# A gated linear recurrence with its decay taken as an exponential, and its gates kept as tanh, in a two-block transformer kernel

## The chip, the core and the metric

The kernel runs on one core of one Trainium2 chip. The metric is the device time of one execution in microseconds (us). TensorE (PE) does the matrix products, ScalarE (ACT) the activation functions and copies, VectorE (DVE) the elementwise work and scans, GpSimd (POOL) one kind of subtraction, SyncE (SP) starts the loads. Every engine works through its own queue in order, and the engines meet only at semaphores.

## What is computed

The program is a chain of blocks over 256 tokens of width 1024: a hybrid mixer with a gated FFN, a recurrent mixer, two expert layers, an attention mixer. The change lies in the recurrent mixer alone:

```python
xb, gb = jnp.split(h @ in_w, 2, axis=-1)
xb = causal_depthwise_conv(xb, conv_w, conv_b)
r = sigmoid(einsum('bsnc,ncd->bsnd', xblk, ra_w) + ra_b)
i = sigmoid(einsum('bsnc,ncd->bsnd', xblk, ri_w) + ri_b)
log_a = -8.0 * softplus(-lam) * r
a = jnp.exp(log_a)
u = jnp.sqrt(-jnp.expm1(2.0 * log_a)) * (i * xb)
hs = scan(h_t = a_t * h_{t-1} + u_t)
y = hs * gelu(gb);  return y @ out_w
```

The width of the recurrence is 1408 channels, so 11 tiles of 128 channels by 256 tokens (`RT` is 11).

## The kernel before

Weights are float32 and every product is made in three passes: a weight tile is split into a `high` part (rounded to float32r) and a `low` part (the rest). SP loads a tile of 128x1024 into one of four slots of `ring`. ACT copies it to `high` (line 1439, called through `ahead`), POOL subtracts to get `low` (line 1767), and PE multiplies (line 787): 16 matmuls with `high`, 8 with `low`. There are three buffers for split tiles, so the splitting runs at most three tiles ahead of PE.

In the recurrent stage PE goes, for each tile j from 0 to 10, through the product x_j, the two gate products of tile j - 2 (`lru_gates`, line 794, into the PSUM tensor `ms`, four banks in turn), and the product g_j. After the loop come the gates of tiles 9 and 10, then 48 matmuls of one column for a later stage (`sum_mods`), and then the output product `lru_out`, whose first two half tiles wait until 8 tiles of y are done, the third until all 11 are.

DVE does the causal convolution of x_j (`lru_conv`, four operations, ended by a memset that signals), then `lru_low(j - 6)`, `lru_coefficients(j - 2)` and `lru_scan(j - 5)`. After the loop it does the coefficients of tile 9, scans and lows of tiles 6 to 8, the coefficients of tile 10, and the rest. PE's gate products of tile j wait for the convolution of tile j + 1 and for the coefficients of tile j - 2 (semaphore `lru_gates_used`).

ACT does for each j the splits, `lru_high(j - 6)` (the rounded copy of a finished y), `lru_act(j - 2)` (the gate functions), the evacuation of g_j (line 1448), and after tiles 2, 5, 8 and 10 `lru_roots`, a square root and a gelu over the tiles finished so far. At the end it does the gate functions of tiles 9 and 10, two splits for `lru_out`, `lru_high` of 5 to 8, the last roots, and `lru_high` of 9 and 10.

The decay is written without an exponential: with t = tanh(4 * softplus(-lam) * r), the kernel uses a = 2 / (1 + t) - 1 and sqrt(1 - a*a) = 2 * sqrt(t) / (1 + t). The factor `c5` comes from `lru_rate`, a chain of small operations on DVE over 128x11, which stands in front of the third tile of the FFN's first product, long before the recurrent stage. `c3` in it is softplus(-lam). `S.settle()` waits for the engine's own last result; `S.did` signals it. `ts`, `tt` and `stt` are DVE's tensor_scalar, tensor_tensor and scalar_tensor_tensor, recorded under lines 1803, 1800 and 1806.

## Time and profile before

| | |
|---|---|
| median of 3 runs | 2595.98 us |
| lowest, highest | 2595.3, 2599.94 us |
| the profiled execution | 2597.65 us |
| its span | 2595.9 us |
| PE busy | 2484.1 us, 96% |
| DVE busy | 1758.1 us, 68% |
| ACT busy | 1225.7 us, 47% |
| POOL busy | 1227.1 us, 47% |
| recurrent stage, with its output product | about 570 to 717 us of the span |

All times of the trace are microseconds from the start of the span. A row of the timeline shows the start, the length, the engine, the line, the operation, and in brackets how long the engine sat idle in front of it and what ended that. Matmul ends are modelled, so the busy share of PE is no measure of its peak.

### The profile page before, as it was taken

Reading aid. Unit: us, or ns where it says so; the run is one execution under the profiler, and the core shown is the slowest. Engines: PE = TensorE matmul, PEld = TensorE weight load, DVE = VectorE, ACT = ScalarE, POOL = GpSimd, SP = SyncE. Lnnn points to the kernel's source line nnn. Section 1 sums busy time; section 2 is a strip of 40 time slices with the busy share of each in tenths; the row PEclk is TensorE's granted clock in tenths of the full one; section 3 lists DMA queues with packets and bytes.
Section 4 is the critical chain, followed back from the end, with each engine's and each line's share of the span. In section 5 each row is a group of like instructions: output and inputs, shape, how many; then the busy total and the mean of one; then the engine's idle time right before and its main releaser. Section 6 shows DMA issues by size and latency. Waiting matters only on the chain.

```text
span 2595.9 us, 46935 instructions
## 1 busy us (share of the span) xinstructions
PE 2484.1 (96%) x18074; PEld 2295.9 (88%) x18074; DVE 1758.1 (68%) x3289; ACT 1225.7 (47%) x2091; POOL 1227.1 (47%) x506
## 2 busy tenths in 40 slices
PE   7899899989799999999999999999999999999999
PEld 7899899979789999998888888888999999888887
DVE  4558553467619969996767765651996899655555
ACT  5325433446445544444444444544545444454544
POOL 4437577745459987771000004446898777200000
PEclk8899899989899999999999997999999999999999
DMA  4325576743245565556777763334556555566664
GB/s 159 98 72 171 205 261 238 293 180 121 89 144 179 181 185 155 155 155 222 257 253 258 259 227 98 106 99 154 171 171 187 155 155 156 176 191 193 190 192 146
DMA packets 125918, 457.93 MB, mean 176 GB/s; under 512 B 13968, under 2 KB 15376, under 8 KB 125584
## 3 DMA queue, kind: packets, MB, share of 16 engines
q1 hardware_dynamic: 125424, 450.73, 54.1%
q10 hardware_dynamic: 288, 4.33, 0.4%
q8 instruction: 145, 2.38, 0.4%
q14 instruction: 61, 0.50, 0.1%
HBM read 453.95 MB, written 1.05 MB: 175 GB/s over the span
## 4 chain that ended last, share of the span: by engine, by line
PE 78%; DVE 7%; POOL 6%; issue 6%; ACT 3%; DMA 1%; SPq 0%; POOLq 0%; DVEq 0%; ACTq 0%
PE ms L1257 27%; PE mm L787 21%; PE mm L1217 19%; POOL low L1767 6%; PE ms L1238 3%; PE ms L794 1%; DMA ring<-w_ple_gate 1%; PE mm L794 1%; DVE hs L1806 1%; PE mm L802 1%; PE mm L900 1%; DVE scratch L1806 1%; DVE work L1800 0%; PE ms L999 0%; DVE work L1806 0%
## 5 line engine op out<-in xcount | busy, mean ns | idle before, releaser
L1767 POOL TENSOR_TENSOR low<-ring,high 128x1024 fp32r<-128x1024 f32 (+2 forms) x502 | 1226.9, 2456 | 1002.7 <-ACT high L1439 844.6
L1646 ACT ACTIVATE high<-ring 128x1024 fp32r<-128x1024 f32 x506 | 535.9, 1059 | 357.0 <-PE ms L1257 325.9
L1217 PE MATMUL mm<-hs,high 128*128 128x256 f32 x4096 | 521.8, 280 | 3.4 <-ACT high L1439 3.4
L1257 PE MATMUL ms<-high,wts 128*128 128x512 f32 x2048 | 511.1, 392 | 0.0
L1217 PEld LDWEIGHTS mm<-hs,high 128*128 128x128 f32 x4096 | 488.2, 188 | 3.8 <-issue 3.8
L2313 DVE TENSOR_TENSOR low<-ring,high 128x1024 fp32r<-128x1024 f32 x256 | 313.3, 1225 | 248.2 <-ACT high L1646 248.2
L1257 PEld LDWEIGHTS ms<-high,wts 128*128 128x128 f32 x2048 | 384.2, 188 | 83.3
L787 PE MATMUL mm<-hs,high 128*128 128x256 f32 x2608 | 346.9, 288 | 4.6 <-DVE parts L1800 4.4
L1439 ACT ACTIVATE high<-ring 128x1024 fp32r<-128x1024 f32 (+2 forms) x252 | 258.0, 1030 | 184.1 <-PE mm L787 111.1
L787 PEld LDWEIGHTS mm<-hs,high 128*128 128x128 f32 x2608 | 326.4, 196 | 9.1 <-issue 7.5
L1217 PE MATMUL mm<-hs,low 128*128 128x256 f32 x2048 | 276.1, 277 | 11.9 <-POOL low L1767 11.8
L1257 PE MATMUL ms<-low,wts 128*128 128x512 f32 x1024 | 275.7, 391 | 3.0 <-DVE low L2313 3.0
L1217 PEld LDWEIGHTS mm<-hs,low 128*128 128x128 f32 x2048 | 251.9, 188 | 14.6 <-POOL low L1767 14.5
L1257 PEld LDWEIGHTS ms<-low,wts 128*128 128x128 f32 x1024 | 192.1, 188 | 46.2 <-DVE low L2313 3.8
L787 PE MATMUL mm<-hs,low 128*128 128x256 f32 x1304 | 179.0, 280 | 0.4 <-POOL low L1767 0.4
L1654 ACT ACTIVATE mm<-mm 128x256 f32<-128x256 f32 (+47 forms) x148 | 39.6, 267 | 269.5 <-PE mm L1217 269.5
L787 PEld LDWEIGHTS mm<-hs,low 128*128 128x128 f32 x1304 | 164.6, 191 | 0.7 <-POOL low L1767 0.7
L2278 DVE TENSOR_TENSOR onehots<-onehots,ms 128x512 bf16<-128x512 bf16 x256 | 162.8, 676 | 0.0
L1448 ACT ACTIVATE work<-mm 128x256 f32<-128x256 f32 (+2 forms) x145 | 60.3, 417 | 204.9 <-PE mm L787 167.9
L1656 ACT ACTIVATE work<-mm 128x256 f32<-128x256 f32 (+17 forms) x248 | 79.7, 321 | 152.6 <-PE mm L1217 152.5
L787 PE MATMUL mm<-parts,high 128*128 128x256 f32 x896 | 126.8, 294 | 15.9 <-DVE parts L1800 10.3
L787 PEld LDWEIGHTS mm<-parts,high 128*128 128x128 f32 x896 | 117.0, 198 | 18.6 <-DVE parts L1800 10.8
(316 smaller groups left out, 2796.1 us busy)
## 6 DMA issues: line engine op xcount, KB each, us to landing
ring<-w_peer_experts SPq DMA_DIRECT2D x512, 512.0 KB, 3.6
work<-w_mod SPq DMA_DIRECT2D x48, 512.0 KB, 4.6
ring<-w_late_mods SPq DMA_DIRECT2D x48, 512.0 KB, 4.6
ring<-w_ffn_up SPq DMA_DIRECT2D x44, 512.0 KB, 3.8
ring<-w_peer_q SPq DMA_DIRECT2D x32, 512.0 KB, 3.6
ring<-w_fox_in SPq DMA_DIRECT2D x32, 512.0 KB, 3.6
ring<-w_lru_in SPq DMA_DIRECT2D x22, 512.0 KB, 3.6
ring<-w_gates SPq DMA_DIRECT2D x16, 512.0 KB, 3.6
```

Source lines behind the costliest of these rows:

```text
L787: ins = pe.matmul(dst, l, r_, start=first and s_ == 0 and k == 0, stop=last and s_ == 2 and k == rows - 1, skip_group_check=True)
L794: ins = pe.matmul(dst, a, b, start=first and i == 0, stop=i == len(pairs) - 1, skip_group_check=True)
L1217: ins_ = pe.matmul(mm[:, s_ % BANKS, 0:T], w_[:, k * P:(k + 1) * P], hs[:, b_, k, :], start=pass_ == 0 and k == 0, stop=pass_ == 2 and k = ...
L1238: ins_ = pe.matmul(ms[:, 2 + i % 2, t * P:(t + 1) * P], onehot[:, i % 2, 3, t, :], onehot[:, i % 2, third, t, :], start=third == 0, stop=t ...
L1257: ins_ = pe.matmul(ms[:, 2 * c + half, :], wts[:, s_ % 3, b_, c * P:(c + 1) * P], v_[:, half * 512:(half + 1) * 512], start=s_ == 0 and pa ...
L1439: act.activation(high[0:rows, q % CUT, 0:width], ring[0:rows, n_ % RAW, 0:width], ACT.Copy) \
L1448: S.did(act.activation(dst, src, func), taken(n))
L1646: act.activation(high[:, (q0 + i) % CUT, :], ring[:, n_ % RAW, :], ACT.Copy) \
L1656: ins = act.activation(placed[:, s_, at:T], src[:, at:T], ACT.Gelu)
L1767: pool.tensor_tensor(low[0:rows, cut_slot, 0:width], ring[0:rows, raw_slot, 0:width], high[0:rows, cut_slot, 0:width].bitcast(F32), ALU.su ...
L2278: dve.tensor_tensor(onehot[:, k % 2, s], onehot[:, k % 2, 2], third(s), ALU.mult)
L2313: dve.tensor_tensor(low[:, q % CUT, :], ring[:, n % RAW, :], high[:, q % CUT, :].bitcast(F32), ALU.subtract).then_inc(sem("low_done"), 1)
```

## The change

The gates stay as tanh. With tr = tanh(z/2), the sigmoid is (1 + tr)/2, so the decay is a = exp(-4c - 4c*tr) with c = softplus(-lam): one ACT Exp with the same column as scale and bias (`lruc` column block 5, now times -4). It is made on ACT beside the tanh of the root, t = tanh(2c + 2c*tr), and goes straight into `la`. Since 1 + a = 2 / (1 + t), the factor in front of the input is sqrt(t/4) * (1 + a) * (1 + ti) * x, with ti the tanh of the input gate. DVE makes (1 + ti) * x in place in PSUM and multiplies by (1 + a). Three small operations in `lru_rate` make the new columns.

```diff
@@ lru_act
-                S.did(act.activation(lr[:, j, :], lru_gate(0, j), ACT.Sigmoid, bias=v("ra_b", j, j + 1)))
+                S.did(act.activation(lr[:, j, :], lru_gate(0, j), ACT.Tanh, bias=lruc[:, 6, j:j + 1], scale=0.5))
                 act.wait_ge(sem("lru_gated"), 2 * j + 2)
-                S.did(act.activation(lru_gate(1, j), lru_gate(1, j), ACT.Sigmoid, bias=v("ri_b", j, j + 1)))
-                S.settle()
-                S.did(act.activation(lt[:, j, :], lr[:, j, :], ACT.Tanh, scale=lruc[:, 5, j:j + 1]), "lru_tanh")
+                S.did(act.activation(lru_gate(1, j), lru_gate(1, j), ACT.Tanh, bias=lruc[:, 7, j:j + 1], scale=0.5))
+                S.settle()
+                S.did(act.activation(lt[:, j, :], lr[:, j, :], ACT.Tanh, bias=lruc[:, 8, j:j + 1],
+                                     scale=lruc[:, 8, j:j + 1]))
+                S.did(act.activation(la[:, j, :], lr[:, j, :], ACT.Exp, bias=lruc[:, 5, j:j + 1],
+                                     scale=lruc[:, 5, j:j + 1]), "lru_decay")
@@ lru_roots
-                act.wait_ge(sem("lru_t_read"), e + 1)
-                S.did(act.activation(lt[:, first:e + 1, :], lt[:, first:e + 1, :], ACT.Sqrt), "lru_root")
+                S.settle()
+                S.did(act.activation(lt[:, first:e + 1, :], lt[:, first:e + 1, :], ACT.Sqrt, scale=0.25), "lru_root")
@@ lru_rate
-                ts(c5, c3, 4.0, None, ALU.mult, None, "lru_rate")
+                ts(lruc[:, 6, :], v("ra_b"), 0.5, None, ALU.mult)
+                ts(lruc[:, 7, :], v("ri_b"), 0.5, None, ALU.mult)
+                ts(lruc[:, 8, :], c3, 2.0, None, ALU.mult)
+                ts(c5, c3, -4.0, None, ALU.mult, None, "lru_rate")
@@ lru_coefficients
-                dve.wait_ge(sem("lru_tanh"), j + 1)
-                r_, i_ = lru_gate(0, j), li[:, j, :]
-                ts(lr[:, j, :], lt[:, j, :], 1.0, None, ALU.add, None, "lru_t_read")
-                S.settle()
-                S.did(dve.reciprocal(r_, lr[:, j, :]))
-                tt(i_, lru_gate(1, j), lc[:, j, :], ALU.mult)
-                S.settle()
-                stt(i_, r_, 2.0, i_, ALU.mult, ALU.mult)
-                ts(la[:, j, :], r_, 2.0, -1.0, ALU.mult, ALU.add, "lru_gates_used")
+                dve.wait_ge(sem("lru_decay"), j + 1)
+                gate = lru_gate(1, j)
+                stt(gate, gate, 1.0, lc[:, j, :], ALU.add, ALU.mult)
+                S.settle()
+                stt(li[:, j, :], la[:, j, :], 1.0, gate, ALU.add, ALU.mult, "lru_gates_used")
```

ACT's queue at the end of the loop, from the evacuation of g_10 to the gate functions of tile 10. Lines 1598 and 1599 are the root and the gelu (1601 and 1602 after the change); 1583, 1585 and 1587 are the gate functions and the tanh of the root, 1589 after the change is the Exp. Before:

```order
L1448 ACTIVATE work<-mm 128x256
L1598 ACT_TABLE_LOAD
L1598 ACTIVATE work<-work 128x768
L1599 ACT_TABLE_LOAD
L1599 ACTIVATE work<-work 128x768
L1583 ACT_TABLE_LOAD
L1583 ACTIVATE work<-ms,vec 128x256
L1585 ACTIVATE ms<-ms,vec 128x256
L1587 ACTIVATE work<-work,lruc 128x256
L1583 ACTIVATE work<-ms,vec 128x256
L1585 ACTIVATE ms<-ms,vec 128x256
L1587 ACTIVATE work<-work,lruc 128x256
```

After:

```order
L1602 ACT_TABLE_LOAD
L1602 ACTIVATE work<-work 128x768
L1583 ACTIVATE work<-ms,lruc 128x256
L1585 ACTIVATE ms<-ms,lruc 128x256
L1587 ACTIVATE work<-work,lruc 128x256
L1589 ACT_TABLE_LOAD
L1589 ACTIVATE work<-work,lruc 128x256
L1583 ACTIVATE work<-ms,lruc 128x256
L1585 ACTIVATE ms<-ms,lruc 128x256
L1587 ACTIVATE work<-work,lruc 128x256
L1589 ACTIVATE work<-work,lruc 128x256
```

One activation is added for each tile, and the table load behind the gelu has moved from the first gate function to the Exp. In the whole stage there are 12 table loads in both programs.

DVE's queue from the coefficients of tile 9 through the scan of tile 6 (lines 2196 and 2198 are the scan itself). Before:

```order
L1803 TENSOR_SCALAR work<-work 128x256
L2183 RECIPROCAL ms<-work 128x256
L1800 TENSOR_TENSOR work<-ms,work 128x256
L1806 SCALAR_TENSOR_TENSOR work<-ms,work 128x256
L1803 TENSOR_SCALAR work<-ms 128x256
L1800 TENSOR_TENSOR work<-work 128x256
L2196 SCALAR_TENSOR_TENSOR work<-work 128x256
```

After, from the scan of tile 8 and the low of tile 7 through the coefficients of tile 10:

```order
L1803 TENSOR_TENSOR work<-work 128x256
L2198 SCALAR_TENSOR_TENSOR work<-work 128x256
L1803 TENSOR_TENSOR work<-work 128x256
L1803 TENSOR_TENSOR parts<-work,parts 128x256
L1809 SCALAR_TENSOR_TENSOR ms<-ms,work 128x256
L1809 SCALAR_TENSOR_TENSOR work<-work,ms 128x256
```

Five operations of a coefficient step have become two; scans and lows stand as they stood. The queues of PE and SP are the same in both programs, and POOL's in its operations.

## Rows read from the trace of the kernel before

**Rows 1.** Windows: length, busy of PE, PEld, DVE, ACT, POOL, PEclk, DMA share, GB/s
```profile
660.00:680.00 20.00, 11.39 (x75) 11.13 (x76) 16.83 (x27) 11.71 (x18) 4.83 (x2) 0.68 0.12 37
```

**Rows 2.** Timeline of PE in the recurrent stage; L794 are gate products
```profile
615.12 2.75 PE L794 MATMUL ms<-work 128*128 128x256 f32 x12
...
631.41 2.75 PE L794 MATMUL ms<-work 128*128 128x256 f32 x12
...
639.37 1.21 PE L787 MATMUL mm<-hs,low 128*128 128x256 f32 x8 [0.36 <-POOL low L1767]
...
649.22 2.86 PE L794 MATMUL ms<-work 128*128 128x256 f32 x12 [0.59 <-DVE tiny L2174]
...
656.53 2.86 PE L794 MATMUL ms<-work 128*128 128x256 f32 x12 [1.71 <-DVE tiny L2174]
660.07 1.97 PE L794 MATMUL ms<-work 128*128 128x256 f32 x8 [0.67 <-DVE work L1803]
...
675.94 3.79 PE L787 MATMUL mm<-parts,high 128*128 128x256 f32 x16 [8.55 <-DVE parts L1800]
```

**Rows 3.** Timeline of DVE: first operation of a coefficient step, first of the next scan
```profile
649.42 0.29 DVE L1803 TENSOR_SCALAR work<-work 128x256 f32<-128x256 f32 x1
...
652.74 0.43 DVE L1800 TENSOR_TENSOR work<-work 128x256 f32<-128x256 f32 x1
```

**Rows 4.** Groups by form, DVE, 580 to 684: busy, mean ns, idle before
```profile
L2183 DVE RECIPROCAL ms<-work 128x256 f32<-128x256 f32 x11 | 19.4, 1761 | 0.4
...
L1806 DVE SCALAR_TENSOR_TENSOR work<-ms,work 128x256 f32<-128x256 f32 x11 | 4.7, 424 | 0.4
```

**Rows 5.** Groups of ACT: busy, mean ns, idle before
```profile
L1587 ACT ACTIVATE work<-work,lruc 128x256 f32<-128x256 f32 x11 | 5.6, 509 | 0.4
...
L1592 ACT ACTIVATE parts<-work 128x256 fp32r<-128x256 f32 x11 | 4.6, 415 | 30.6 <-DVE work L1800 30.6
```

**Rows 6.** Timeline of ACT from the evacuation of g_10 to the high of tile 5
```profile
655.95 0.36 ACT L1448 ACTIVATE work<-mm 128x256 f32<-128x256 f32 x1
656.33 1.28 ACT L1598 ACT_TABLE_LOAD   x1
...
663.19 0.46 ACT L1583 ACTIVATE work<-ms,vec 128x256 f32<-128x256 f32 x1
...
664.44 1.99 ACT L1439 ACTIVATE high<-ring 128x1024 fp32r<-128x1024 f32 x2
666.33 0.40 ACT L1592 ACTIVATE parts<-work 128x256 fp32r<-128x256 f32 x1
```

**Rows 7.** Timeline of DVE: scan of tile 6, lows of tiles 5 and 7
```profile
666.65 1.54 DVE L1800 TENSOR_TENSOR work<-work 128x256 f32<-128x256 f32 x1
668.22 2.71 DVE L2196 TENSOR_TENSOR_SCAN work<-work 128x256 f32<-128x256 f32 x1
...
671.31 0.42 DVE L1800 TENSOR_TENSOR parts<-work,parts 128x256 fp32r<-128x256 f32 x1
...
675.47 0.42 DVE L1800 TENSOR_TENSOR parts<-work,parts 128x256 fp32r<-128x256 f32 x1
```

**Rows 8.** Timeline of POOL beside it
```profile
665.55 4.83 POOL L1767 TENSOR_TENSOR low<-ring,high 128x1024 fp32r<-128x1024 f32 x2 [13.46 <-ACT high L1439]
```

**Rows 9.** Timelines of ACT and DVE: the last roots, and the scan behind them
```profile
676.01 1.28 ACT L1598 ACT_TABLE_LOAD   x1
...
679.97 0.43 DVE L1800 TENSOR_TENSOR work<-work 128x256 f32<-128x256 f32 x1 [0.65 <-ACT work L1599]
```

**Rows 10.** Timelines of DVE, PE and POOL at the end of lru_rate
```profile
334.97 0.17 DVE L1803 TENSOR_SCALAR lruc<-lruc 128x11 f32<-128x11 f32 x1
335.05 0.43 DVE L1800 TENSOR_TENSOR mm<-mm,work 128x256 f32<-128x256 f32 x1
...
336.54 3.39 PE L787 MATMUL mm<-hs,high 128*128 128x256 f32 x16 [4.41 <-DVE parts L1800]
...
337.84 2.38 POOL L1767 TENSOR_TENSOR low<-ring,high 128x1024 fp32r<-128x1024 f32 x1 [4.77 <-ACT high L1439]
```

More of the change, by code:

```diff
@@ L454, in build @@
         csilu = sb("csilu", [P, KD])
-        lruc = sb("lruc", [P, 6, RT])
+        lruc = sb("lruc", [P, 10, RT])
         tiny = sb("tiny", [P, 512])
```

## The prediction, made before the changed kernel ran

> **What bounds the kernel now.** I began with the page: PE is busy for 96% of the span, so only those stretches can give anything in which PE waits. The windows showed one around the recurrent stage: from 660 to 680 PE is busy 11.39 us of 20 and DVE 16.83 [rows 1]. I then read PE's own timeline there, and the reader is to look at the brackets [rows 2]. Until 637 PE never waits: two rounds of x, gates and g take 16.29 us (615.12 to 631.41). After that DVE is late: 0.59 and 1.71 us of waiting for convolutions, 0.67 for a coefficient step, and 8.55 us until the lows of tiles 0 to 7 are done. There is also one wait of 0.36 us for a split tile. Nothing else in the stage can be won, and of these waits the last is much the longest. So the question is not how much DVE saves but when the low of tile 7 comes, which lets PE go at 675.94.
>
> **Part 1, the coefficient step on DVE.** Before it takes 3.32 us (649.42 to 652.74) [rows 3], of which the reciprocal is 1.76 [rows 4]. After it is two operations of 0.42 us [rows 4] with some 0.03 between, 0.9 us. That frees 2.4 us a tile, 27 us over 11 tiles. Most of it falls where DVE is not waited for. What it surely does is end the backlog from 637 on: a round of DVE (convolution 2.2, low 0.4, coefficients 0.9, scan 1.7, with up to 2.7 of stalls) fits into 8.15.
>
> The new operations read one operand from PSUM and one from SBUF. I have no row of one that writes PSUM in place; the bounds are 0.42 (this row) and the 0.54 of a convolution's first operation, so 1.3 us more in all at worst, off the path but for 0.1 of tile 9. I take 0.42.
>
> **Part 2, ACT.** The Exp has two column operands, scale and bias. The tanh with one takes 0.509, a copy with none 0.415 [rows 5]; so I estimate 0.60 with two. The root's tanh goes from 0.51 to 0.60 too. Since neighbours overlap by some 0.1, a tile costs ACT 0.6 us more, 6.6 over the stage. Table loads stay 12. In most rounds ACT waits for PE or for DVE, which hides this; on the way to the low of tile 7 nothing hides it for tiles 9 and 10.
>
> The Trainium skill (ScalarE: Activation LUTs, What ACT_TABLE_LOAD costs) says that each such column operand adds some 93 ns; the rows show 94, so the price of the new form would be the same by either.
>
> **Part 3, the way to the low of tile 7.** Step by step:
> - PE. Without the waits the gates of tile 8 begin 16.29 after 631.41, at 647.70, instead of 649.22: 1.52 earlier. The gates of tile 9 began at 656.53 behind a wait of 1.71; without it they begin at 656.53 - 1.71 - 1.52 = 653.30 [rows 2]. The product g_10 stands just in front of them.
> - ACT. Its evacuation of g_10 came at 655.95, late because ACT had been waiting for a product of DVE. It now comes at about 653.3, 2.65 earlier. From there ACT's queue is solid: roots and gelu of tiles 6 to 8 with the gate functions of tile 9 (656.33 to 663.19), gate functions of tile 10 (to 664.44), two splits (to 666.33), then the high of tile 5 [rows 6]. That is 10.38 us, and two tiles at 0.6 make it 11.6. So the high of tile 5 begins at 664.9 and ends at 665.3.
> - DVE. The Exp of tile 9 is done at about 661.3 (663.3 - 2.65 + 0.7), its coefficients at 662.2, the scan of tile 6 at 663.9. Then DVE waits for that high until 665.3. Before, DVE came to this point at 671.31, behind everything else [rows 7].
> - The stalls. Operations of DVE that read two SBUF operands stand still while POOL works: the multiply at 666.65 took 1.54 instead of 0.43, and the scan at 668.22 took 2.71 instead of 0.69 [rows 7], under a pair of POOL operations from 665.55 to 670.38 [rows 8]. The pair begins when the first split of `lru_out` is done, so it moves by 2.65 - 1.2 to 664.1, its first half ends at 666.5, and the second at 668.9. The low of tile 5, ready at 665.3, is held to 666.7. The multiply of tile 7 then meets the second half and ends at 669.1. From there no POOL work is left. Unhindered, low 5 to low 7 is 4.16 us (671.31 to 675.47) and the first 0.97 of it are the low and the multiply, so 3.19 remain: low 7 begins at 672.3 against 675.47, **3.2 us earlier**.
>
> The Trainium skill (SBUF — State Buffer, Terms) says that DVE and GpSimd share one pair of SBUF ports under a lock held for the whole instruction, and that the loser is blocked. The rows agree. By that rule the sum is -3.2; were the stalls chance, it would be the -6.0 of the second rival.
>
> **Part 4, the tail.** The last roots begin behind the high of tile 8 at 676.01, and the scan of tile 9 waits for them to 679.97 [rows 9]. The high of tile 8 hangs on the scan of tile 8, so this moves by the same 3.2. The shorter coefficient step of tile 10 lies in this wait and gives nothing. After it the work is unchanged. PE has its wait in front of `lru_out` longer, not shorter: gates and column sums end at about 662.3 and it starts at 672.4. The 16 matmuls at 675.94 took 3.79 us for the usual 1.98, as the granted clock was at half there [rows 1, 2]; that cost remains.
>
> **Part 5, lru_rate.** Here DVE is waited for: PE stood 4.41 us until 336.54 for the operation behind this chain [rows 10]. The three added operations are of 0.17 us, but follow without a settle, like 334.97 and 335.05, so 0.08 each: **+0.25 us** straight on PE's path. A POOL operation beside them could hold each for up to its own 2.4 us, 7 in all, but POOL is idle there until 337.84, since its split comes from ACT, which waits for the same DVE work [rows 10]. I take 0.25.
>
> **Sum.** -3.2 + 0.25 = -2.95. The profiled execution took 2597.65 with a span of 2595.9, so its like would be 2594.7. It lies 1.7 above the median; taken from the median of 2595.98 the forecast is **2593.0 us**.
>
> **Rivals.**
> - *No stalls (17%).* POOL's pair and DVE's operations miss each other. Then low 5 goes at 665.3, low 7 4.16 later at 669.4: -6.0 + 0.25, **2590.2**. Against it: the two are both set off by ACT within 1.2 us of each other, and the pair lasts 4.83.
> - *One more stall (12%).* A third operation meets POOL, as where the scan lost 2.0 [rows 7]: -1.0 in all, **2595.0**.
> - *It does not do what it says (6%).* PE's last wait is set by ACT's queue in a way that I took too short: the load between tanh and Exp, or a dearer Exp, eats the 2.65. Then the low of tile 7 comes as before, **2596.2**.
> - *ACT becomes the bound, slower (5%).* A round without roots costs ACT some 4.8 us, one with roots and a reload 10.4, against PE's 8.15. If the three split buffers do not absorb these 2.2 us, PE waits in three rounds, and each wait can bring the half clock, as at 336.54 (3.39 for 1.98 us) [rows 10]: 3 x 3.6 - 2.95 = +7.9, **2603.9**. For it: the one wait of 0.36 for POOL [rows 2] came behind such a round. Against it: in that round ACT was late because it waited for DVE, which is now gone, and with three buffers it can run about a tile (24 matmuls, a third of a round) ahead. It decides from where ACT's lag passes that lead.
>
> **How the numbers follow.** The forecast has 60%. What a measurement of this kernel can tell from no change is about 0.2%, 5.2 us; so under 2590.8 counts as faster and over 2601.2 as slower. Faster is most of the first rival and the lower edge of the forecast's own spread (the runs before differ by 4.6, and the half clock costs some 2 us that may fall otherwise): 20%. Slower is the last rival and a little of disturbance: 6%. The rest is 74%. The range goes from 2589.0, under the case without stalls, to 2597.0, above the case in which nothing is won; the last rival and an odd run are left out.
>
> **What the trace would show.** Right: PE's waits of 0.59, 1.71 and 0.67 are gone; coefficient steps take 0.9 us; Exp takes 0.60; the first `lru_out` matmuls begin near 673.0 (675.94 - 3.2 + 0.25), behind an idle of PE of some 10 us instead of 8.55; DVE waits for an ACT high in front of a low, and one or two of its operations there last near 2 us. Wrong: PE's brackets name POOL `low` or ACT in the middle of the stage; the wait at 336.54 grows by over 1 us; or low 7 begins under 670, which would say that the stalls were misjudged.

## The result, and the profile after

The changed kernel takes 2660.86 us (median of 4 runs, 2658.92 to 2661.25) against 2597.96 for the kernel before in the same comparison: 1.0242 times as long, with an interval of 1.0226 to 1.0258. That is 63 us slower, where 3 us faster was forecast with a range up to 2597.0. The sign was wrong and the size was off by a factor of twenty, so the first question is where in the program the time went.

It did not go into the recurrent stage. Here is PE's timeline of that stage after the change, to be read against [rows 2]. The first row is the first gate product of the stage, which I take as the stage's zero from here on, since the stage begins at other times in other executions:

```profile
592.61 1.89 PE L794 MATMUL ms<-work 128*128 128x256 f32 x8
...
647.92 2.18 PE L787 MATMUL mm<-hs,high 128*128 128x256 f32 x16 [0.54 <-ACT high L1439]
...
660.55 2.86 PE L794 MATMUL ms<-work 128*128 128x256 f32 x12 [0.61 <-DVE tiny L2180]
...
667.67 4.58 PE L794 MATMUL ms<-work 128*128 128x256 f32 x20 [1.39 <-DVE tiny L2180]
...
687.20 3.78 PE L787 MATMUL mm<-parts,high 128*128 128x256 f32 x16 [8.16 <-DVE parts L1803]
```

From the first gate product to the first product of `lru_out` it is 94.59 us. Before it was 675.94 - 583.39 = 92.55, with the row of its first gate product:

```profile
583.39 1.89 PE L794 MATMUL ms<-work 128*128 128x256 f32 x8
```

So the stage is 2 us longer, of 63. The rest is everywhere. The page's groups of PE show it, first the kernel before, then the one after (busy us in all, mean ns of one, idle time before):

```profile
PE 2484.1 (96%) x18074; PEld 2295.9 (88%) x18074; DVE 1758.1 (68%) x3289; ACT 1225.7 (47%) x2091; POOL 1227.1 (47%) x506
...
L1217 PE MATMUL mm<-hs,high 128*128 128x256 f32 x4096 | 521.8, 280 | 3.4 <-ACT high L1439 3.4
L1257 PE MATMUL ms<-high,wts 128*128 128x512 f32 x2048 | 511.1, 392 | 0.0
```

```profile
PE 2555.8 (96%) x18074; PEld 2352.3 (88%) x18074; DVE 1744.2 (66%) x3259; ACT 1231.6 (46%) x2102; POOL 1226.6 (46%) x506
...
L1217 PE MATMUL mm<-hs,high 128*128 128x256 f32 x4096 | 543.8, 284 | 3.4 <-ACT high L1439 3.4
L1257 PE MATMUL ms<-high,wts 128*128 128x512 f32 x2048 | 521.7, 397 | 1.0 <-DVE wts L2306 1.0
```

The same 18074 matmuls take 71.7 us more; PE's idle time (span less busy) falls from 111.8 to 103.1, and 71.7 - 8.7 = 63.0 is the whole difference of the spans. Lines 1217 and 1257 are the expert layers; line 1217 runs from 782.6 us of the span to 2233.2, where the change does nothing. The two timelines there, at the full granted clock, show each matmul a little slower. Before, then after:

```profile
1003.76 2.09 PE L1217 MATMUL mm<-hs,high 128*128 128x256 f32 x16
1005.68 1.07 PE L1217 MATMUL mm<-hs,low 128*128 128x256 f32 x8
1006.60 0.84 PE L1238 MATMUL ms<-onehots 128*128 128x128 bf16 x12
```

```profile
1003.10 2.16 PE L1217 MATMUL mm<-hs,high 128*128 128x256 f32 x16
1005.10 1.12 PE L1217 MATMUL mm<-hs,low 128*128 128x256 f32 x8
1006.06 0.84 PE L1238 MATMUL ms<-onehots 128*128 128x128 bf16 x12
```

The 24 matmuls on `hs` go from 2.84 us (1003.76 to 1006.60) to 2.96 (1003.10 to 1006.06), while the 12 on `onehots` take 0.84 in both. A clock would have slowed both kinds. The measure that I use from here on is the **pitch**: the mean distance between the starts of neighbouring matmuls of one group in the trace, those at half clock left out. It went from 114.5 to 119.9 ns for line 1217 on `hs` and `high`, and from 229.1 to 234.3 for line 1257. Over all groups on `hs`, `parts` and `wts` the pitches make 77 us (4096 x 5.4 ns is 22 of them); the 71.7 measured are a little less. At half clock the matmuls did not get slower: the pitch of line 787 on `hs` is 213 ns there in both traces, and the 16 at 687.20 above took 3.78 us, those in [rows 2] 3.79. These matmuls are counted in the 77.

What the change does to the whole program is a line that the diff ahead of the prediction left out, since it seemed to be room for columns and nothing more:

```diff
-        lruc = sb("lruc", [P, 6, RT])
+        lruc = sb("lruc", [P, 10, RT])
```

`lruc` grows from 264 to 440 bytes a partition, and every tensor allocated behind it (`tiny`, `work` with `parts` in it, `hs`, `wts`) moves by 160 bytes in SBUF. `ring`, `high` and `low` stand ahead of it and stay. In bytes from the partition's start, as the two programs lay them out, `high` is at 17536 in both, and `hs` at 199488 before and 199648 after.

### The profile page after: what moved, and what is told of

It reads as the page before. It is cut to its first block, busy times and chain, and to the rows that moved or that the text cites. A ratio compares the mean times of both kernels' runs of the same rounds, so it can differ in the third digit from the quotient of the medians.

```text
span 2658.9 us, 46916 instructions
## 1 busy us (share of the span) xinstructions
PE 2555.8 (96%) x18074; PEld 2352.3 (88%) x18074; DVE 1744.2 (66%) x3259; ACT 1231.6 (46%) x2102; POOL 1226.6 (46%) x506
## 4 chain that ended last, share of the span: by engine, by line
PE 76%; DVE 7%; POOL 6%; issue 5%; ACT 3%; DMA 1%; SPq 0%; POOLq 0%; DVEq 0%; ACTq 0%
PE ms L1257 27%; PE mm L787 20%; PE mm L1217 19%; POOL low L1770 6%; PE ms L1238 3%; DMA ring<-w_ple_gate 1%; DVE work L1809 1%; DVE hs L1809 1%; DVE work L1803 1%; PE mm L802 1%; PE mm L794 1%; PE mm L900 1%; PE ms L794 1%; DVE scratch L1809 1%; ACT high L1439 1%
## 5 line engine op out<-in xcount | busy, mean ns | idle before, releaser
L1217 PE MATMUL mm<-hs,high 128*128 128x256 f32 x4096 | 543.8, 284 | 3.4 <-ACT high L1439 3.4
L1257 PE MATMUL ms<-high,wts 128*128 128x512 f32 x2048 | 521.7, 397 | 1.0 <-DVE wts L2306 1.0
L1217 PEld LDWEIGHTS mm<-hs,high 128*128 128x128 f32 x4096 | 507.4, 188 | 3.8 <-issue 3.8
L787 PE MATMUL mm<-hs,high 128*128 128x256 f32 x2608 | 359.3, 291 | 4.4 <-DVE parts L1803 3.8
L787 PEld LDWEIGHTS mm<-hs,high 128*128 128x128 f32 x2608 | 337.7, 196 | 8.8 <-issue 6.4
L1217 PE MATMUL mm<-hs,low 128*128 128x256 f32 x2048 | 287.6, 282 | 7.4 <-POOL low L1770 7.4
L1257 PE MATMUL ms<-low,wts 128*128 128x512 f32 x1024 | 281.6, 397 | 2.9 <-DVE low L2315 2.9
L1217 PEld LDWEIGHTS mm<-hs,low 128*128 128x128 f32 x2048 | 263.5, 188 | 9.5 <-POOL low L1770 9.5
L787 PE MATMUL mm<-hs,low 128*128 128x256 f32 x1304 | 185.9, 285 | 0.3 <-POOL low L1770 0.3
L787 PEld LDWEIGHTS mm<-hs,low 128*128 128x128 f32 x1304 | 170.8, 192 | 0.8 <-POOL low L1770 0.7
L787 PEld LDWEIGHTS mm<-parts,high 128*128 128x128 f32 x896 | 118.2, 196 | 16.4 <-DVE parts L1803 9.8
```

What stands on the lines that cost most here:

```text
L787: ins = pe.matmul(dst, l, r_, start=first and s_ == 0 and k == 0, stop=last and s_ == 2 and k == rows - 1, skip_group_check=True)
L1217: ins_ = pe.matmul(mm[:, s_ % BANKS, 0:T], w_[:, k * P:(k + 1) * P], hs[:, b_, k, :], start=pass_ == 0 and k == 0, stop=pass_ == 2 and k = ...
L1257: ins_ = pe.matmul(ms[:, 2 * c + half, :], wts[:, s_ % 3, b_, c * P:(c + 1) * P], v_[:, half * 512:(half + 1) * 512], start=s_ == 0 and pa ...
```

## The experiments

The two theories of the first round were **placement** (the 63 us come from where `hs`, `parts` and `wts` lie, whatever the arithmetic is) and **work** (the new instructions on ACT and DVE hold PE up). Within placement it was then **absolute** (a tensor's own address decides) against **distance** (the address of one operand of a matmul relative to that of the other). A matmul has two operands: the weights, which are loaded ahead of it, and the moving operand, of which the count of columns is told here (256 or 512).

### e1_room_only: the room without the change

```diff
 (the kernel before)
-        lruc = sb("lruc", [P, 6, RT])
+        lruc = sb("lruc", [P, 10, RT])
```

> The kernel before, with nothing changed but the size of lruc: 10 blocks of columns instead of 6, four of them unused. In the trace of the changed kernel the matmuls that read hs follow each other at some 120 ns instead of 113.4, from the first microseconds on, long before any changed operation runs. Theory P (placement): the larger lruc moves tiny, work, parts, hs and wts by 160 bytes in SBUF, from a multiple of 64 bytes to 32 bytes past one, and TensorE streams its moving operand slower from there. Then this kernel takes 2658 to 2664 us, like the changed one. Rival W (work): the new operations or the new order on ScalarE and VectorE slow TensorE; then it takes 2595 to 2600 us.

Measured: 2660.33 us (2657.02 to 2661.54), 1.0249 times the kernel before (1.0234 to 1.0264). The group in its page is that of the changed kernel to 0.1 us:

```profile
L1217 PE MATMUL mm<-hs,high 128*128 128x256 f32 x4096 | 543.7, 284 | 3.4 <-ACT high L1439 3.4
```

No instruction differs from the kernel before, so the whole loss is placement.

### e2_same_place: the change without the room

The new columns go into blocks 0, 1 and 2 of `lruc`, which nobody reads any more by then (the softplus is in block 3):

```diff
 (the changed kernel)
-        lruc = sb("lruc", [P, 10, RT])
+        lruc = sb("lruc", [P, 6, RT])
...
-                ts(lruc[:, 6, :], v("ra_b"), 0.5, None, ALU.mult)
-                ts(lruc[:, 7, :], v("ri_b"), 0.5, None, ALU.mult)
-                ts(lruc[:, 8, :], c3, 2.0, None, ALU.mult)
+                ts(lruc[:, 0, :], v("ra_b"), 0.5, None, ALU.mult)
+                ts(lruc[:, 1, :], v("ri_b"), 0.5, None, ALU.mult)
+                ts(lruc[:, 2, :], c3, 2.0, None, ALU.mult)
```

> The changed kernel whole, but its three new columns lie in blocks 0, 1 and 2 of lruc, whose old contents are used up by then; lruc keeps its 6 blocks and every tensor its place. Theory P: matmuls on hs go back to 113.4 ns, and only the forecast effects of the arithmetic remain: 2593 to 2596 us, 3 under the kernel before (low of tile 7 some 3.2 us earlier, lru_rate 0.25 longer); 2590 if the stalls of VectorE under GpSimd miss. Rival W: 2655 to 2662 us.

Measured: 2598.11 us (2591.42 to 2601.82, 12 runs), 1.0006 times before (0.9996 to 1.0016), which is 2 us above the 2593 to 2596 that I expected. Placement holds from this side too, and the theory of work falls. It is also the run that puts the prediction's own question, what the arithmetic is worth in the old order, and its answer is nothing that the runs can tell from zero: -1.0 to +4.2 us, where -2.95 was forecast. What became of them is taken up under e9.

### e3_room_pad32: 32 bytes more behind the larger lruc

```diff
 (the changed kernel)
         lruc = sb("lruc", [P, 10, RT])
+        gap = sb("gap", [P, 8])
```

> The changed kernel with lruc of 10 blocks, followed by an unused tensor of 32 bytes a partition. hs then starts at a multiple of 128 bytes (before: 64 past one). Theory P in the form 'multiple of 64 bytes': the time of e2, 2590 to 2597 us. If instead the exact old place matters, or the distance to other tensors, it stays at 2620 to 2662 us. If 128 bytes is the finer rule, it is below e2.

Measured: 2643.24 us (2640.74 to 2648.93), 1.0186 (1.0173 to 1.0199). The loss depends on the bytes themselves: 32 bytes more gave back 17 to 18 of 63 us. It is not a matter of being moved or not.

### e4_hs_moved and e5_all_moved: absolute or distance

```diff
 (e4: the kernel before)
+        gap = sb("gap", [P, 8])
         hs = sb("hs", [P, 2, KD, T], F32R)
```

> The kernel before, with an unused tensor of 32 bytes in front of hs: hs and wts lie 32 bytes past a multiple of 64, while tiny, work and parts stay. Theory P with the moving operand as its carrier: 6144 matmuls of line 1217 and 3912 of line 787 read hs and lose 6 ns each, 3072 of line 1257 read wts and lose some 4: 60 + 12 = 70 less what waits absorb, so 2650 to 2662 us. If it is work or parts that matter (the other engines' traffic), 2595 to 2605 us.

```diff
 (e5: the kernel before)
+        gap = sb("gap", [P, 8])
         ring = sb("ring", [P, RAW, SLOT])
```

> The kernel before with an unused tensor of 32 bytes a partition in front of everything: ring, high, low and all others lie 32 bytes further, and all distances between them stay. So hs lies 352 bytes past a multiple of 512 (before: 320), and high 160 (before: 128). Theory A (absolute place of the moving operand): matmuls on hs follow each other at 118 ns and more as when hs alone moved by 32, 2640 to 2665 us. Theory D (distance between the moving operand and the weights that are loaded beside it): pitch and time stay as before, 114.6 ns, 2594 to 2600 us.

e4 moves `hs` and `wts` (with `slots`, which shares the place of `wts`) by 32 bytes and nothing else: 2643.62 us, 1.0183 (1.0168 to 1.0198). e5 moves `hs` and `wts` by the same 32 bytes, and `high` and all others with them: 2594.28 (8 runs), 1.0002 (0.9991 to 1.0014). In both, `hs` lies at the same address, no multiple of 64. Their pages, e4 first (with the added line of code 1217 has become 1218, and 1257 is 1258):

```profile
L1218 PE MATMUL mm<-hs,high 128*128 128x256 f32 x4096 | 537.2, 284 | 3.4 <-ACT high L1440 3.4
L1258 PE MATMUL ms<-high,wts 128*128 128x512 f32 x2048 | 519.7, 395 | 0.0
```

```profile
L1218 PE MATMUL mm<-hs,high 128*128 128x256 f32 x4096 | 523.1, 280 | 3.4 <-ACT high L1440 3.4
L1258 PE MATMUL ms<-high,wts 128*128 128x512 f32 x2048 | 510.5, 391 | 0.0
```

So the distance between the two operands decides, and the absolute address does not. In e4 `parts` stayed where it was, and so did the pitch of its products (116.2 ns against 116.3): each pair of operands counts by its own distance. (Strictly, these two runs show that the distance to something among `ring`, `high` and `low` counts, as no run moved these against each other. That it is the other operand of the same matmul follows from the products with changed roles below.) The time of e4 is below the 2650 that I expected at least, so I had the size of one step wrong, not its sign.

### e6 to e8, e13 and e14: which distances

All five are e2_same_place with unused bytes ahead of `tiny`: 64, 128, 256, 96 and 224.

```diff
 (e6: e2_same_place)
         lruc = sb("lruc", [P, 6, RT])
+        gap = sb("gap", [P, 16])
```

> The changed arithmetic with lruc of 6 blocks (the run with the same place), and 64 unused bytes in front of tiny, so that work, hs and wts lie 64 bytes further: hs at 384 past a multiple of 512. So far, mean pitch of matmuls on hs by hs's place past a multiple of 512: 320 gave 114.7, 352 gave 118.3, 480 gave 120, 0 gave 118.8. If the place counts by 64 bytes with some places bad, this can go either way; if every place but a few is slow, 2635 to 2660 us; if 64-byte steps are harmless except 192, 2592 to 2600 us.

> As the last one, with 128 bytes: hs at 448 past a multiple of 512. A rule with period 128 (64 past it good, 0 past it bad) gives 114.7 ns and 2592 to 2600 us here, and a slow run for 64 bytes. A rule with period 512 leaves it open, 2592 to 2660 us.

> As the last one, with 256 bytes: hs at 64 past a multiple of 512. A rule with period 128 or 256 gives the fast pitch, 2592 to 2600 us; a rule with period 512 leaves it open.

> The same arithmetic in the same columns as e2_same_place (2598.1), with 96 unused bytes ahead of `tiny`: hs then lies 32 bytes past a multiple of 256 from `high` (288 - 256), a distance that no kernel so far has had. By the theory of distance its 128x256 products on hs and high fall in with those at 0, 64, 96, 128 and 224 bytes (a pitch of 117.5 to 120 ns, 2637 to 2661 us), since 192 is so far the only distance with 114 ns. If instead there is more than one fast distance, the pitch is 114 to 115 ns and the time 2597 to 2600 us.

> As e13_plus96 with 224 unused bytes, so that hs lies 160 bytes past a multiple of 256 from `high`: the neighbour of 192 on the side that no kernel has had (224, on its other side, gave a pitch of 118.2 ns and 2643.6 us). Slow like that neighbour: 117.5 to 120 ns, 2637 to 2661 us. If the fast place is wider than one step of 32 bytes, 114 to 115 ns and 2597 to 2600 us.

These were single runs: 2638.3 (e6), 2637.68 (e7), 2599.2 (e8), and on another chip, where the kernel before took 2591.1, 2634.19 (e13) and 2636.9 (e14). The group of line 1218 in their pages, in the order e6, e7, e8, e13, e14, for e6 with that of line 1258:

```profile
L1218 PE MATMUL mm<-hs,high 128*128 128x256 f32 x4096 | 543.5, 286 | 3.4 <-ACT high L1440 3.4
...
L1258 PE MATMUL ms<-high,wts 128*128 128x512 f32 x2048 | 506.5, 389 | 1.0 <-DVE wts L2307 1.0
```

```profile
L1218 PE MATMUL mm<-hs,high 128*128 128x256 f32 x4096 | 533.7, 282 | 3.4 <-ACT high L1440 3.4
```

```profile
L1218 PE MATMUL mm<-hs,high 128*128 128x256 f32 x4096 | 520.4, 280 | 3.4 <-ACT high L1440 3.4
```

```profile
L1218 PE MATMUL mm<-hs,high 128*128 128x256 f32 x4096 | 532.8, 282 | 3.4 <-ACT high L1440 3.4
```

```profile
L1218 PE MATMUL mm<-hs,high 128*128 128x256 f32 x4096 | 534.5, 283 | 3.4 <-ACT high L1440 3.4
```

The rule with a period of 128 bytes, which the expectation of e7 names, is refuted by its 2637.68 us. e13 and e14 were slow as expected, with times of 3 us and 0.1 us under the range, and pitches inside it or 0.3 ns under it.

Together with the earlier kernels there is now one for each of the eight distances in steps of 32 bytes. In the table the distance is the address of `hs` less that of `high`, modulo 256; `wts` lies at the same distance from `high` as `hs` does in all these kernels. But the operands of line 1257 have the other roles. In the code the second argument of `matmul` is the weights and the third the moving operand:

```python
 (line 1217)
ins_ = pe.matmul(mm[:, s_ % BANKS, 0:T], w_[:, k * P:(k + 1) * P], hs[:, b_, k, :],
...
 (line 1257)
ins_ = pe.matmul(ms[:, 2 * c + half, :], wts[:, s_ % 3, b_, c * P:(c + 1) * P],
                 v_[:, half * 512:(half + 1) * 512], start=s_ == 0 and pass_ == 0,
...
```

`w_` and `v_` are tiles of `high` or `low`. So in line 1217 `hs` moves, and in line 1257 `high` or `low` moves, with 512 columns, and `wts` is the weights. The profile has it so too. In line 1257 the weight loads are of 128 columns, the matmuls of 512:

```profile
L1257 PEld LDWEIGHTS ms<-high,wts 128*128 128x128 f32 x2048 | 385.2, 188 | 94.8 <-DVE wts L2306 1.4
```

The expectations of e4 and e12 take `wts` for the moving operand; that is wrong, and it turns the sign of its distance. Some products of an early stage (line 787) have these changed roles with 256 columns: `high` or `low` moves, `hs` is the weights. The table has all three kinds, each with the address of its moving operand less that of its weights ("moving less weights"), modulo 256.

| `hs` less `high` | kernel | pitch, `hs` moving, 256 columns (line 1217) | moving less weights, when `high` moves | pitch, `high` moving over `hs`, 256 columns | pitch, `high` moving over `wts`, 512 columns | time against before |
|---|---|---|---|---|---|---|
| 0 | e6 | 119.9 ns | 0 | 119.7 ns | 226.8 ns | +43.7 us |
| 32 | e13 | 117.2 | 224 | 118.4 | 233.3 | +43.1 |
| 64 | e7 | 117.5 | 192 | 115.1 | 233.3 | +43.1 |
| 96 | after, e1 | 119.9 | 160 | 118.2 | 234.3 | +62.9, +64.4 |
| 128 | e3 | 118.7 | 128 | 118.6 | 232.6 | +47.3 |
| 160 | e14 | 117.6 | 96 | 119.6 | 233.4 | +45.8 |
| 192 | before, e5 | 114.5, 114.8 | 64 | 116.6 | 229.1, 228.9 | 0, -0.3 |
| 192 + 256 | e8 | 114.1 | 64 | 116.7 | 229.1 | +4.6 |
| 224 | e4 | 118.2 | 32 | 117.3 | 233.2 | +47.7 |

Read by moving less weights, the two kinds with 256 columns agree within 1 ns at each of the eight distances: 119.9 and 119.7 at 0, 117.2 and 117.3 at 32, 117.5 and 116.6 at 64, 119.9 and 119.6 at 96, 118.7 and 118.6 at 128, 117.6 and 118.2 at 160, 114.5 and 115.1 at 192, 118.2 and 118.4 at 224. Kernel e7 shows it best: its `hs` products are slow, and its products with changed roles are the fastest of their kind. From one start to the next, with 12 matmuls between (8 on `high`, 4 on `low`), it is 1.42 us in the kernel before and 1.36 in e7:

```profile
115.22 1.10 PE L787 MATMUL mm<-high,hs 128*128 128x256 f32 x8
...
116.64 1.10 PE L787 MATMUL mm<-high,hs 128*128 128x256 f32 x8
```

```profile
113.61 1.07 PE L788 MATMUL mm<-high,hs 128*128 128x256 f32 x8
...
114.97 1.07 PE L788 MATMUL mm<-high,hs 128*128 128x256 f32 x8
```

So it is the distance between the two operands of one matmul, with its sign, that counts. For the 256-column products a moving operand 192 bytes past its weights is the one fast place, by 2.4 ns or more on `hs` (114.8 against 117.2); 256 bytes on, it is fast again. The products on `parts` gain less from it (115.3 to 116.4 ns in the kernels at 192, 117.3 and more at the others). The kernel before lay on it, and a change to the size of any small tensor between `low` and `hs` would have cost it 43 us or more in seven cases of eight. The 512-column products behave otherwise: 0 is best for them (226.8), a moving operand 64 bytes past its weights next (229.1), and 192 is as slow as the rest (233.3). The +4.6 of e8 is one run, within the scatter of single runs (its twin without the 256 bytes, e2, had 2591.42 to 2601.82). Five of the nine rows are single runs and some have the changed arithmetic, so their times are good to some 5 us; the pitches are means over more than 2500 matmuls, and over 231 where `high` moves over `hs`.

### e9_scan_first: why the arithmetic gained nothing

In e2 the distance from the first gate product to the first `lru_out` product is 675.77 - 581.61 = 94.16 us, 1.6 more than before; forecast was 3.2 less. The loop of DVE, ACT and POOL in e2 shows why. DVE, from one product of a scan (the third operation of a multiply, scan and product) to the next:

```profile
618.06 0.42 DVE L1803 TENSOR_TENSOR work<-work 128x256 f32<-128x256 f32 x1
...
621.88 2.54 DVE L1803 TENSOR_TENSOR work<-work 128x256 f32<-128x256 f32 x1
624.46 2.77 DVE L2198 TENSOR_TENSOR_SCAN work<-work 128x256 f32<-128x256 f32 x1
627.26 0.42 DVE L1803 TENSOR_TENSOR work<-work 128x256 f32<-128x256 f32 x1
```

and beside it ACT and POOL:

```profile
618.51 0.42 ACT L1595 ACTIVATE parts<-work 128x256 fp32r<-128x256 f32 x1 [4.79 <-DVE work L1803]
```

```profile
621.79 4.90 POOL L1770 TENSOR_TENSOR low<-ring,high 128x1024 fp32r<-128x1024 f32 x2 [4.31 <-ACT high L1439]
```

The product of a scan (618.06) releases ACT, which has stood 4.79 us for it. ACT then does the high of y, its four gate functions and a split (to 621.7), the split releases POOL at 621.79, and exactly there DVE has come to the multiply and the scan, which both read two SBUF operands. They take 2.54 and 2.77 instead of 0.42 and 0.69, so the next product comes at 627.26, 9.20 after the last. The loop feeds itself: DVE's stall delays the product, the product delays ACT and POOL, and POOL comes when DVE is at the next multiply. 9.20 us a round is more than PE's 8.15. Before, the reciprocal stood in that window. With one SBUF operand and its result in PSUM it took 1.76 us beside POOL too (the mean of 11 is 1761 ns [rows 4]), and by the end of the coefficient step half of POOL's pair was over, so that at most one of the two operations lost its 1.6 to 2.2 us a round. Two rounds of the kernel before:

```profile
616.57 2.75 DVE L2196 TENSOR_TENSOR_SCAN work<-work 128x256 f32<-128x256 f32 x1
...
625.49 2.01 DVE L1800 TENSOR_TENSOR work<-work 128x256 f32<-128x256 f32 x1
```

So in such a round the 2.4 us that the change frees a tile (part 1, with the size as forecast) went into a second stall of 2.1. There are three such rounds in e2; the others between them have one stall. Over the whole stage the operations of DVE that took more than 0.15 us over their own time lost 10.1 us before (6 operations) and 21.8 in e2 (11 operations). From the end of one scan to the end of the scan four tiles on it is 35.6 us in e2 (8.9 a round) and 34.6 before.

The test is to break the loop. e9 puts the scan ahead of the coefficients in the loop, so that the product comes sooner after the convolution, and changes nothing else:

```diff
 (e2_same_place, the loop over j on DVE)
-                if j >= 2:
-                    lru_coefficients(j - 2)
                 if j >= 5:
                     lru_scan(j - 5)
+                if j >= 2:
+                    lru_coefficients(j - 2)
```

> The changed arithmetic in the old place, and in DVE's loop the scan of tile j - 5 in front of the coefficients of tile j - 2. In the run with the same place a round in the middle of the stage went: ScalarE waits 4.8 us for the product of a scan, does its high, the gate functions and a split, GpSimd starts its pair at that moment (4.9 us), VectorE has just finished the short coefficients and stands with multiply and scan under the pair (2.5 and 2.8 us instead of 0.43 and 0.69), so the next product is late again. Theory S (the freed time is lost at GpSimd's work, in a loop that feeds itself): with the scan ahead of the coefficients, which wait for ScalarE, the loop is broken; ScalarE's waits of 4.8 us and PE's waits of 0.9 to 1.4 us in front of the last gate products vanish, 2592 to 2596 us with the same tail. Rival L (ScalarE's longer queue is the bound, its waits are only slack): PE's waits stay, 2596 to 2600 us.

Measured: 2594.55 us (12 runs), 0.9990 (0.9981 to 0.9999). All waits of PE in the middle of the stage are gone, and no scan is held up any more. Stalls remain, 14.2 us on 8 operations (multiplies and lows), but PE waits for none of them before the tail. These rows of its timeline are the stage's zero, the gates of tile 8, those of tile 9 with 10, and the first `lru_out` product:

```profile
585.29 1.89 PE L794 MATMUL ms<-work 128*128 128x256 f32 x8
...
649.61 2.75 PE L794 MATMUL ms<-work 128*128 128x256 f32 x12
...
655.02 4.48 PE L794 MATMUL ms<-work 128*128 128x256 f32 x20
...
674.77 3.78 PE L787 MATMUL mm<-parts,high 128*128 128x256 f32 x16 [7.71 <-DVE parts L1803]
```

The last comes 89.48 us after the first: 3.07 less than before and 4.7 less than e2. This is the size of the gain that the prediction had put on the change alone. The whole time is in line with it, though its interval is wide: 0.9990 is -2.6 us, -0.3 to -4.9. How much the order alone would have given the old arithmetic was not run.

### e10_order: what the tail is worth

The prediction left the tail's order alone. The work of tiles 6 to 8 does not need to stand behind the gate functions of tile 9 (which wait for a square root, a gelu and their table loads on ACT). DVE scans 6 to 8 first, then makes the coefficients of tile 9 and the lows; ACT makes the highs of 5 to 8 before the two splits of `lru_out`, so that POOL's pair comes later:

```diff
 (e9_scan_first)
-            ahead("lru_out", 0, 1)
             for k in range(5, 9):
                 lru_high(k)
+            ahead("lru_out", 0, 1)
...
-            lru_coefficients(RT - 2)
             for k in range(6, 9):
                 lru_scan(k)
+            lru_coefficients(RT - 2)
+            for k in range(6, 9):
                 lru_low(k - 1)
```

> As the last one, and the tail reordered too: VectorE does the scans of tiles 6 to 8 before the coefficients of tile 9, ScalarE the highs of tiles 5 to 8 before the two splits for the output product (whose GpSimd work held up the lows). Theory S: the low of tile 7 comes near 665 instead of 675.3, limited then by the first split, and the output product starts 8 to 10 us earlier, 2586 to 2591 us. Rival L: ScalarE's queue from the roots on is as long as before, at most 3 us are won, 2592 to 2598 us.

Measured: 2584.68 us (2584.26 to 2590.16, 5 runs), 0.9962 (0.9949 to 0.9975), 1.3 us under the range of theory S. The two edits, DVE's and ACT's, were not run one by one. Zero and first `lru_out` product:

```profile
582.52 1.89 PE L794 MATMUL ms<-work 128*128 128x256 f32 x8
...
664.47 3.75 PE L787 MATMUL mm<-parts,high 128*128 128x256 f32 x16 [0.36 <-DVE parts L1803]
```

81.95 us instead of 92.55, and the long wait is 0.36. The product that waits for all 11 tiles came 96.31 after the zero, against 106.13 before; 9.8 is the gain of the whole, and the time agrees (2596.15 x 0.0038 = 9.9). (The traced run of e10 was 4.7 above its median.)

### e11_old_math_order: the same orders with the old arithmetic

The kernel before with the two orders of e10, to tell whether the change has a share in that gain.

> The kernel before, with its reciprocal and sigmoids, in the same two new orders. If the order alone gives the gain, it is as fast as the changed arithmetic in that order, 2586 to 2592 us. If VectorE's 27 us of reciprocals and copies matter once the stalls are gone (a round of VectorE is 2.2 + 0.4 + 1.7 + 3.3 = 7.6 us of PE's 8.15 before any stall), it stays 3 to 8 us behind it, 2590 to 2597 us.

Measured: 2591.59 us (12 runs), 0.9982 (0.9973 to 0.9992): 4.7 better than before, 6.9 behind e10 (5.6 by the means). Both expected ranges hold this time, and it is the distance to e10 that speaks for the second: within 3 to 8 us. The rows point at the longer coefficient step as what holds it back:

```profile
624.96 2.45 DVE L1803 TENSOR_SCALAR work<-work 128x256 f32<-128x256 f32 x1
```

```profile
653.36 2.86 PE L794 MATMUL ms<-work 128*128 128x256 f32 x12 [2.36 <-DVE tiny L2174]
...
665.95 3.46 PE L794 MATMUL ms<-work 128*128 128x256 f32 x8 [2.42 <-DVE work L1803]
```

The first operation of the coefficient step takes 0.29 alone [rows 3] and 2.45 here, under POOL, and PE again waits for convolutions and a coefficient step. This operation reads one SBUF operand only, so the stalls are not limited to operations with two. The order did its part in the tail, where PE's last wait is 1.86 instead of 8.55. So the new arithmetic is worth some 5 to 7 us in the new order, and nothing in the old one. (The traced run of e11 was 5.9 above its median, so its rows show a dear case.)

### e12_wts64: the placement used

The table says that the experts' second product (line 1257) prefers a distance of 0. e12 puts 64 bytes between `hs` and `wts`, which leaves `hs` at 192:

```diff
 (e10_order)
         hs = sb("hs", [P, 2, KD, T], F32R)
...
+        gap = sb("gap", [P, 16])
         wts = sb("wts", [P, 3, 2, T], F32R)
```

> The changed arithmetic in the new orders, with 64 unused bytes between hs and wts. Distances of the moving operand to the weights, past a multiple of 256: hs keeps 192, wts goes from 192 to 0. In the run with everything moved by 64, the matmuls on wts followed each other at 226.8 ns instead of 229 and those on hs at 119.9. If each operand goes by its own distance, this kernel has 226.8 on wts and 114.7 on hs, and is 3072 x 2.2 ns = 7 us faster than the same kernel without the gap, 2579 to 2585 us. If the two hang together, it is not.

Measured: 2576.39 us (2570.08 to 2580.43, 6 runs), 0.9922 (0.9908 to 0.9937), 8.3 under e10, 2.6 under the expected range, and the fastest of all. The pitch with `wts` is 226.7, that with `hs` moving still 114.5:

```profile
L1218 PE MATMUL mm<-hs,high 128*128 128x256 f32 x4096 | 521.9, 280 | 3.4 <-ACT high L1440 3.4
...
L1258 PE MATMUL ms<-high,wts 128*128 128x512 f32 x2048 | 506.2, 389 | 0.0
```

3072 matmuls at 2.3 ns less are 7 us, so the table accounts for nearly all of it. With e4 it also shows that each pair of operands counts by itself: here `wts` alone changed its distance to `high`, and the products on `hs` kept their pitch.

## Why the prediction was wrong, point by point

- **The step that failed** is one that the prediction made without a term: it priced the edits one by one and closed with "After it the work is unchanged". The larger `lruc` was an edit too, and got no line, no bound and no rival. It alone costs 64 us (e1), and the changed kernel without it is at 2598.11 (e2). A second step failed beside it, which the 63 us hide: the stalls of part 1, without which the -3.2 of part 3 is not reached.
- **What bounds the kernel.** "Only those stretches can give anything in which PE waits" holds for gains that come from other engines. It is no bound on losses: PE is busy for 96% of the span, and 2 to 5% more for most of its matmuls (71.7 us) is six times all its waits in the recurrent stage before (0.36 + 0.59 + 1.71 + 0.67 + 8.55 [rows 2]). Nor is it a bound on gains from placement: e12 won 8.3 us over e10, 7 of them by a shorter pitch in products that PE does not wait for.
- **Part 1, the coefficient step.** The size was right: 0.43 and 0.42 us for the two operations, the one in PSUM at the low end of its bounds. What failed is the sentence that a round "fits into 8.15" with up to 2.7 us of stalls. The stalls are 4.2 in e2 (2.54 and 2.77 for 0.42 and 0.69), and the prediction's own 5.2 us of work with 4.2 more is 9.4, near the 9.20 of the round shown. I had read the stalls from the rows of the kernel before, where the reciprocal kept DVE out of POOL's way for part of the pair, and then took the reciprocal away. The stage got 1.6 us longer instead of 3.2 shorter.
- **Part 2, ACT.** Right. In e2 the Exp takes 0.59 to 0.60 and the tanh with two columns 0.60, as these groups of the changed kernel show:

```profile
L1587 ACT ACTIVATE work<-work,lruc 128x256 f32<-128x256 f32 x11 | 6.6, 601 | 0.4
L1589 ACT ACTIVATE work<-work,lruc 128x256 f32<-128x256 f32 x11 | 6.5, 591 | 0.0
```

- **Part 3, the way to the low of tile 7.** Its chain was right where its start was: with the zero at the first gate product, gates of tile 8 were forecast at 647.70 - 583.39 = 64.31 and those of tile 9 at 69.91; e9, in which the premise of no waits holds, has 64.32 and 69.73, and its wait for the low of tile 7 ends 3.07 us earlier than before, against 3.2. That is a check of the chain in another order of DVE's loop than the one it was written for. In the kernel as changed the premise did not hold. The stalls under POOL's pair in the tail were met as forecast too. In e2 the low of tile 5 took 1.42 and the multiply of tile 7 2.35:

```profile
668.21 1.42 DVE L1803 TENSOR_TENSOR parts<-work,parts 128x256 fp32r<-128x256 f32 x1 [1.39 <-ACT parts L1595]
669.77 2.35 DVE L1803 TENSOR_TENSOR work<-work 128x256 f32<-128x256 f32 x1
```

  The rule of the Trainium skill (SBUF — State Buffer, Terms) that the prediction leaned on, a lock on a shared pair of ports for a whole instruction, agrees with all of these rows. It was applied in the tail, and not in the loop, where it decided.
- **Part 4.** The last wait moved with the low of tile 7, as forecast (106.13 after the zero before, 103.06 in e9). The start of `lru_out` is given there as 672.4; 675.94 - 3.2 is 672.7.
- **Part 5, lru_rate.** +0.25 was forecast. PE's wait there is 4.80 us in e2, e9 and e10 (4.09 in e12), and 4.41 [rows 10], 4.59 (e5) and 4.58 (e11) with the old arithmetic in the same placement, so +0.2 to +0.4 in the first three.
- **The rivals.** None of them names placement. The one on the slower side (ACT becomes the bound) is not what made the kernel slow. A small part of it is there: behind the round with roots PE waits 1.01 us in e2 for ACT's `high` and 0.32 for POOL's `low`, where it waited 0.36 before. But ACT stands up to 4.8 us in a round waiting for DVE, and in e9, with ACT's work as long, these waits are gone.
- **What was said to show it wrong.** PE's brackets do name ACT `high` in the middle of the stage in the changed kernel (0.54), as that part warned; but none of the signs it lists looks outside the stage. A look at the mean of a matmul in groups that the change does not touch would have found the cause at once.

## What to carry to other kernels

A change that alters the size of any tensor in SBUF moves all that are allocated behind it, so compare the addresses of TensorE's operands before and after, and the pitch of matmuls that the change doesn't touch; keep the placement fixed (reuse columns, or pad) when the arithmetic is what you want to judge. Where VectorE and GpSimd stall each other, look at what the removed operation did for the timing of the ones behind it: a slow operation that is not held up can be the cover under which another engine's work passes. Before counting an engine's saved time as gained, follow who releases whom around the loop, as the round time is set by the loop and not by the engine's own work.

## What the hardware showed that was not expected

TensorE's rate depends on the distance in SBUF between the moving operand and the weights (the address of the moving one less that of the weights), modulo 256 bytes as far as tried (192 and 192 + 256 alike). On float32r products with 128x128 weights and 256 columns the pitch of line 1217 is 114.1 to 114.8 ns at a distance of 192 and 117.2 to 119.9 at the other seven steps of 32 bytes, and products with the roles of the two tensors changed follow the same list within 1 ns. With 512 columns it is 226.7 to 226.8 at 0, 228.9 to 229.1 at 64, and 232.6 to 234.3 elsewhere. This is at the full clock. At half clock the pitch of line 787 on `hs` is 213 ns in all sixteen kernels. The pattern of single pitches is regular, at distance 0 nearly all are 120, at 96 they run through 116, 117, 118, 121, 123 and 125. The bfloat16 products on `onehots` and those of line 794 did not change, but both of their operands lie in one tensor, so their distance did not change either. The 128-column products of line 1195 did change their distance (`ring` moves over weights in `work`), and stayed at 111.7 ns in every kernel.

The mechanism was not measured. The Trainium skill (TensorE: Matmul & The Clock Gate, Step-by-step: what each phase is for) says that TensorE has two independent read ports into SBUF, one for the moving operand and one for the weights, and that loading the next weights takes nothing from the running matmul. The runs here do not agree in full: the two reads matter to each other by their distance, at 2 to 5%. Whether that is their meeting in some part of the memory is open, and so is why 192 is best with 256 columns and 0 with 512, and what a distance that is no multiple of 32 does; no run had one.
